# A fused network on one NeuronCore: modulation blocks ahead of first products, a ring filled two blocks further, and RWKV's first mix without the difference

## The reference, cut to what matters

```python
for i in range(DEPTH_2):                       # 4
    shift, scale, gate = modulation(c, mod_w[i], mod_b[i])     # silu(c) @ mod_w[i] + mod_b[i]
    h = modulate(rmsnorm(x, norm_g[i]), shift[:, None], scale[:, None])
    ...                                        # the same with c_ctx for the context
    x = x + gate[:, None] * y

def rwkv_features(h, proj, with_out):
    xx = centred_shift(h) - h                  # 0.5 * (left + right neighbour) - h
    lerp = lambda n: h + xx * mu[n]
    k = lerp(2) @ w_k
    ...                                        # r from lerp(0), w from 1, v from 3, a from 4, g from 5
```

## Time and profile before

| | |
|---|---|
| runs | 3016.09, 3008.73, 3015.09 us; median 3015.09 |
| the profiled execution | 3009.6 us, its span 3007.8 us, mean granted clock 0.943 |
| PE busy | 2640.9 us, 88% of the span |
| DVE, ACT, POOL busy | 50%, 37%, 25% |
| ring blocks | 311 issues in the page, 512 KB each, 3.8 us (median) from issue to landing |
| store and reload of the stream X | 3072 KB each; the store takes 9.7 us to landing |
| HBM | 203.04 MB read, 36.70 MB written |

### The profile page before, as it was taken

How to read it: one execution, slowest core, us unless ns; L and a number is a source line. 1 busy time by engine, 2 the same in 40 slices (tenths; PEclk the granted TensorE clock), 3 DMA queues, 4 the chain that set the end, 5 groups by cost and what they waited for, 6 DMA issues and landing times. The chain is left out here.

```text
span 3007.8 us, 66771 instructions
## 1 busy us (share of the span) xinstructions
PE 2640.9 (88%) x28836; PEld 2003.8 (67%) x28836; DVE 1511.2 (50%) x2661; ACT 1127.2 (37%) x1763; POOL 762.1 (25%) x438
## 2 busy tenths in 40 slices
PE   8897899979799996888888887789999999898987
PEld 5675577847578785676767776568778655476755
DVE  4634478883642313545555544334550166525995
ACT  4533332232352333444444443234432344423323
POOL 2322200002112125545444441122223300032111
PEclk9998999999789897999999999889999999999998
DMA  4214253334434441111111100441312200044421
GB/s 149 77 57 139 86 156 100 98 90 130 152 138 165 152 142 62 40 40 51 35 35 51 45 15 24 173 162 50 126 57 71 62 1 1 29 158 138 141 88 56
DMA packets 83663, 266.38 MB, mean 89 GB/s; under 512 B 11824, under 2 KB 12848, under 8 KB 82992
## 3 DMA queue, kind: packets, MB, share of 16 engines
q1 hardware_dynamic: 74160, 236.97, 24.8%
q10 hardware_dynamic: 9216, 25.17, 2.1%
HBM read 203.04 MB, written 36.70 MB: 80 GB/s over the span
## 5 line engine op out<-in xcount | busy, mean ns | idle before, releaser
L373 PE MATMUL ps<-h_parts_conv,w_parts_one 128*128 128x512 f32 x3168 | 582.1, 344 | 43.0 <-DVE h_parts_conv L359 32.3
L373 PEld LDWEIGHTS ps<-h_parts_conv,w_parts_one 128*128 128x128 f32 x3168 | 494.7, 191 | 137.6 <-issue 43.3
L373 PE MATMUL ps<-scratch_scan 64*64 64x64 f32 (+1 forms) x15936 | 376.1, 236 | 87.3 <-issue 48.0
L373 PEld LDWEIGHTS ps<-scratch_scan 64*64 64x64 f32 x15936 | 338.0, 137 | 132.8 <-issue 87.8
L441 POOL TENSOR_TENSOR w_parts_rwkv_out<-ring,w_parts_rwkv_out 128x1024 fp32r<-128x1024 f32 x80 | 191.1, 2391 | 807.1 <-ACT w_parts_rwkv_out L370 807.1
L441 POOL TENSOR_TENSOR w_parts_one<-ring,w_parts_one 128x1024 fp32r<-128x1024 f32 x82 | 202.8, 2475 | 716.9 <-ACT w_parts_one L370 716.9
L370 ACT ACTIVATE scratch_scan<-ps 128x384 f32<-128x384 f32 x560 | 241.3, 493 | 369.5 <-PE ps L373 225.1
L367 DVE SCALAR_TENSOR_TENSOR scratch_conv<-scratch_conv,vec 128x256 f32<-128x256 f32 (+1 forms) x672 | 337.4, 575 | 0.5
L373 PE MATMUL ps<-h_parts_attn,w_parts_rwkv_out 128*128 128x512 f32 (+1 forms) x1536 | 331.0, 374 | 5.8 <-DVE h_parts_attn L367 5.8
L373 PEld LDWEIGHTS ps<-h_parts_attn,w_parts_rwkv_out 128*128 128x128 f32 x1536 | 265.3, 190 | 65.0 <-issue 14.9
L373 PE MATMUL ps<-h_parts_block,w_parts_one 128*128 128x512 f32 x960 | 241.2, 409 | 19.3 <-DVE h_parts_block L359 17.1
(11 more groups left out here) (215 smaller groups left out, 3353.1 us busy)
## 6 DMA issues: line engine op xcount, KB each, us to landing
ring<-in_weights SPq DMA_DIRECT2D x311, 512.0 KB, 3.8
rwkv_spill<-scratch_conv ACTq DMA_DIRECT2D x64, 384.0 KB, 2.3
stream<-rwkv_spill SPq DMA_DIRECT2D x64, 384.0 KB, 3.6
scratch_conv<-scratch_conv SPq DMA_DIRECT2D x128, 103.1 KB, 2.2
scratch_conv<-scratch_conv SPq DMA_DIRECT2D x128, 67.4 KB, 2.0
x_spill<-stream SPq DMA_DIRECT2D x2, 3072.0 KB, 9.7
y_spill<-scratch_scan SPq DMA_DIRECT2D x8, 384.0 KB, 4.1
scratch_rwkv_out<-y_spill SPq DMA_DIRECT2D x8, 384.0 KB, 6.4
```

Of the source, the lines that this page charges most:

```text
L373: return nc.tensor.matmul(o, l, r, start=start, stop=stop)
```

## The change

Five things change.

1. `tile_product` takes three numbers, `mods=(front, behind, col)`: so many modulation blocks before the first k-step, then one behind each of the first `behind` k-steps. Numbers (front, behind) by stage: out1 (2, 2), gate1 (2, 0), conv0 (6, 2), convout0 (6, 2), rkvg (4, 4), rwkvout (2, 0), attn_qk (6, 2), attnout (2, 2), conv1 (6, 2). Before, one block stood behind each of the first k-steps: four in out1, gate1, rwkvout, attn_qk and attnout, eight in the others. In gate1 and rwkvout one more pair stands behind a later product; in attn_qk the pairs behind the first two products go. MODS places the blocks in the ring to match, and in gate1 the first two split blocks come ahead of the direct ones.
2. The ring is filled up to START + SLOTS + 2 at the ends of in1, out1, gate1, add_products' stages, attn_g and attnout (not at the ends of conv0, conv1 and rkvg); before, up to START + SLOTS.
3. RWKV's first mix is `LF = h * (1 - mu) + sum * (0.5 * mu)`: ACT writes `h * (1 - mu)` into LF with a scale per channel, DVE adds the second term. The difference is formed for all eight tiles behind the first group.
4. The wait for `normed` before the first turning of values goes.
5. Three semaphores of the convolution layers are shared by both, with a base added to the numbers waited for.

The diff, cut:

```diff
-MODS = {"out1": {1: 4, 3: 2, 5: 2}, "gate1": {3: 4, 5: 2, 7: 2},
+MODS = {"out1": {1: 4, 3: 2, 5: 2}, "gate1": {3: 2, 5: 2, 6: 2, 7: 2},
...
-    stage("gate1", [("w_ple_proj", 0, 0), ("w_ple_proj", 0, 1)] + [("w_ple_gate", 0, m) for m in range(8)])
+    stage("gate1", [("w_ple_gate", 0, m) for m in range(2)] + [("w_ple_proj", 0, m) for m in range(2)] + [("w_ple_gate", 0, m) for m in range(2, 8)])
...
+            mod_blocks(pe, mods[0], mods[2])
             for k in range(DT):
...
-                if k < mods[0]:
-                    mod_blocks(pe, 1, mods[1])
+                if k < mods[1]:
+                    mod_blocks(pe, 1, mods[2])
...
-                R.supply(sp, RINGT, weights, START["out1"] + SLOTS)
+                R.supply(sp, RINGT, weights, START["out1"] + SLOTS + 2)
...
-                    if m in (2, 4):
+                    if m in (2, 3, 4):
                         mod_blocks(pe, 2, 5 * 512)
...
+                def first_mix(k):
+                    v.wait_ge(in_hi, base_shifted + 4 * k + 4)
+                    for j, (a, b, c) in enumerate(HALF):
+                        v.wait_ge(dve_chain.sem, dve_chain.base + dve_chain.n - 1 + j)
+                        stt(LF[:, k, a:b], XX[:, k, a:b], HALFMU[:, k:k + 1], LF[:, k, a:b], ALU.mult, ALU.add).then_inc(l_ready, 1)
+
+                def differences():
+                    for k in range(DT):
+                        for a, b, c in HALF:
+                            n, o = b - a, hoff[c]
+                            dve_chain.inc(stt(XX[:, k, a:b], XX[:, k, a:b], 0.5, HP[:, k, o:o + n], ALU.mult, ALU.subtract))
                     dve_chain.wait(v)
...
                 mod_gain(1, 2)
+                dlink(vts(HALFMU, V("rwkv_mu_2", groups[0][0] * DT, DT), 0.5))
+                vts(RESTMU, V("rwkv_mu_2", groups[0][0] * DT, DT), -1.0, 1.0, ALU.mult, ALU.add).then_inc(rest_ready, 1)
...
+                    for j, (p, q, c) in enumerate(HALF):
+                        a.wait_ge(in_hi, base_shifted + 4 * k + j + 1)
+                        if k == 0:
+                            a.wait_ge(rest_ready, 1)
+                        act(LF[:, k, p:q], HP[:, k, hoff[c]:hoff[c] + q - p], ACT.Copy, scale=RESTMU[:, k:k + 1]).then_inc(in_hi, 1)
...
-                                 mods=(4, MODS_3) if n == 0 else (0, 0))
-                    if n < 2:
-                        mod_blocks(pe, 2, MODS_3)
+                                 mods=(6, 2, MODS_3) if n == 0 else (0, 0, 0))
...
                         if kinds[n - 1][1] == 0:
                             pe.wait_ge(mods_added, 10)
-                            pe.wait_ge(normed, NT_)
```

More of the change, by code:

```diff
@@ L106 @@
 IN_ORDER = [base + m for base in (0, 12, 8, 16, 4, 20) for m in range(4)]
-MODS = {"out1": {1: 4, 3: 2, 5: 2}, "gate1": {3: 4, 5: 2, 7: 2},
+MODS = {"out1": {1: 4, 3: 2, 5: 2}, "gate1": {3: 2, 5: 2, 6: 2, 7: 2},
         "conv0": {1: 8}, "convout0": {1: 8, 3: 2, 4: 2, 5: 2, 6: 2},
-        "rkvg": {1: 8, 11: 2, 13: 2, 15: 2, 16: 2}, "rwkvout": {1: 4, 3: 2, 5: 2},
-        "attn_qk": {1: 6, 2: 2, 11: 2, 13: 2, 15: 2, 17: 2}, "attnout": {1: 4, 6: 2, 10: 2}, "conv1": {1: 8}}
+        "rkvg": {1: 8, 11: 2, 13: 2, 15: 2, 16: 2}, "rwkvout": {1: 2, 2: 2, 3: 2, 5: 2},
+        "attn_qk": {1: 8, 11: 2, 13: 2, 15: 2, 17: 2}, "attnout": {1: 4, 6: 2, 10: 2}, "conv1": {1: 8}}
 def weight_plan():
@@ L452, in part_block_vector, with tile_product @@
                 done["part"] += 1
-        def tile_product(pe, o, width, area=None, start=True, stop=True, fresh=None, used=None, mods=(0, 0)):
+        def tile_product(pe, o, width, area=None, start=True, stop=True, fresh=None, used=None, mods=(0, 0, 0)):
             j = done["take"]
@@ L1011, in _ @@
                         bring(sp, base_hi)
-                    R.supply(sp, RINGT, weights, min(b for b in [*START.values(), NB] if b > START[stage]) + SLOTS)
+                    R.supply(sp, RINGT, weights, min(b for b in [*START.values(), NB] if b > START[stage]) + SLOTS + 2)
                 @block.scalar
@@ L1041, in _ @@
                                      fresh=(split_low, base_low, 1) if split and m == 0 else None,
-                                     mods=(mods[0][3], mods[0][1]) if mods and m == 0 else (0, 0))
+                                     mods=(*mods[0][3], mods[0][1]) if mods and m == 0 else (0, 0, 0))
                         for third, col, rows, _n, later, _at, turn_at in mods:
@@ L1094, in _ @@
                 sp.dma_start(PE_, pT.rearrange("(k p) t -> p k t", p=P)).then_inc(loads, 16)
-                R.supply(sp, RINGT, weights, START["conv0"] + SLOTS)
+                R.supply(sp, RINGT, weights, START["conv0"] + SLOTS + 2)
             @block.tensor
@@ L1102, in _ @@
                     tile_product(pe, PS[:, (m % 2) * 512:(m % 2) * 512 + 512], TX,
-                                 fresh=(split_low, base_low, 1) if m == 0 else None, mods=(4, 5 * 512) if m == 0 else (0, 0))
+                                 fresh=(split_low, base_low, 1) if m == 0 else None, mods=(2, 0, 5 * 512) if m == 0 else (0, 0, 0))
                     if m == 0:
@@ L1206, in two_blocks @@
         z_summed, centred, z_scaled, silued, gated_ = (sem(n) for n in ("z_summed", "centred", "z_scaled", "silued", "gated_"))
[L1208 removed]
+        conv_sems = tuple(sem(n) for n in ("a_read", "b_read", "gate_read", "pe_taps", "taps_added", "padded",
+                                           "s_free", "diag_ready", "stacked"))
         def conv_layer(layer, j_, width):
@@ L1312, in _ @@
                                          fresh=input_fresh if m == 0 and part == 0 else None,
-                                         mods=(8, 5 * 512) if m == 0 and part == 0 else (0, 0))
+                                         mods=(6, 2, 5 * 512) if m == 0 and part == 0 else (0, 0, 0))
                             if m >= 1 and part == 1:
@@ L1430, in conv_layer @@
             add_products(f"convout{j_}", width, lambda m, c: MODL[:, layer, 16 + m, c:c + 1],
-                         2 if j_ == 0 else 0, split=(silu_and_high, gate_and_low), mods=[(3, 4 * 512, MOD_ROWS, 8, (), 0, 1), (4, 5 * 512, MOD_ROWS, 0, (2, 3, 4, 5), 6, 6)] if j_ == 0 else (),
+                         2 if j_ == 0 else 0, split=(silu_and_high, gate_and_low), mods=[(3, 4 * 512, MOD_ROWS, (6, 2), (), 0, 1), (4, 5 * 512, MOD_ROWS, (0, 0), (2, 3, 4, 5), 6, 6)] if j_ == 0 else (),
                          sums=([sa[:, n, 0:width] for n in range(2)], sb_[:, 0, 0:width]))
@@ L1517, in _ @@
                         neighbours(k - 1)
-                        lerp(groups[0][0], k - 1)
+                        first_mix(k - 1)
                     if k >= 2:
@@ L1545, in _ @@
                                      used=h_used if (kind, q, m) == prods[-1] and e + 1 < len(groups) else None,
-                                     mods=(8, 5 * 512) if n == 0 else (0, 0))
+                                     mods=(4, 4, 5 * 512) if n == 0 else (0, 0, 0))
                         n += 1
@@ L2621, in two_blocks @@
                      split=plain_split([YR[:, k, :] for k in range(DT)], TT, lambda k: (in_loaded[k], 16 * (NPAIR + 1))),
-                     bring=bring_back, stream=lambda m: (in_loaded[m], 16 * (NPAIR + 2)), sums=([sq[:, 0, :], sq[:, 1, :]], acc), mods=[(7, 4 * 512, take(256), 4, (2, 4), 5, 6)])
+                     bring=bring_back, stream=lambda m: (in_loaded[m], 16 * (NPAIR + 2)), sums=([sq[:, 0, :], sq[:, 1, :]], acc), mods=[(7, 4 * 512, take(256), (2, 0), (1, 2, 4), 5, 6)])
         NQ, NKV = 16, 8
@@ L2658, in _ @@
                 sp.dma_start(ROPE.rearrange("p a t -> p (a t)"), rope).then_inc(loads, 16)
-                R.supply(sp, RINGT, weights, START["attnout"] + SLOTS)
+                R.supply(sp, RINGT, weights, START["attnout"] + SLOTS + 2)
             @block.tensor
@@ L2898, in _ @@
                 sp.dma_start(X.rearrange("p k t -> p (k t)"), x_dram).then_inc(loads, 16)
-                R.supply(sp, RINGT, weights, START["conv1"] + SLOTS)
+                R.supply(sp, RINGT, weights, START["conv1"] + SLOTS + 2)
             @block.scalar
@@ L2930, in _ @@
                                      fresh=(split_low, base_low + DT * half, 1) if m == 0 else None,
-                                     mods=(4, 4 * 512) if m == half == 0 else (0, 0))
+                                     mods=(2, 2, 4 * 512) if m == half == 0 else (0, 0, 0))
                     if m in (2, 4):
```

27 lines of the change are left out of this document (12 added, 15 removed).

## The result

Four runs of the changed kernel took 2964.77 to 2973.52 us, median 2966.71; beside them the kernel before has a median of 3014.64. The ratio is 0.985, interval 0.984 to 0.987: 1.5% faster. Predicted was 2967. The profiled execution has a span of 2963.6 us (before 3007.8, 44.2 more).

What follows compares the result with a forecast made beforehand. TensorE was taken as the bound, so its standing still was what counted. Stage terms summed to 46.0 us, taken as 45.6, giving 2964.0 from the profiled execution or 2969.5 from the median; forecast 2967, range 2951 to 2986.

Steps and rivals of the forecast that it cites:

- gate1, rwkvout: First products no longer wait for late modulation blocks: gains of 11.8 us in gate1 and 9.1 us in rwkvout.
- no wait for the ring: Sign for gate1: TensorE waits for no ring block, and the third product starts at 300.
- attnout: Four blocks loaded at the stage's start remove the first product's hole of 4.97 us: gain 8.0 us, bounds 6 and 9.5.
- my second case: attnout: TensorE's clock, high when the stage begins, holds, but third weights land behind the stream: gain 8.6 us.
- rkvg's first mix: VectorE's pace per k-step falls from 4.98 to 3.93 us in rkvg's first product: gain 6.9 us, bounds 5 and 8.5.
- attn_v: The needless 3.93 us wait before the first transposition goes, and the next product runs faster: gain 5.4 us.
- attn_qk: Front blocks five and six land behind the 3 MB store and hold k-step 0: loss of 2.3 us.
- conv1: Four blocks run in the hole, two more follow, then k-steps of 0.7: gain 3.4 us, bounds 2 and 4.
- out1: A pair of blocks in the starting hole and an earlier clock: gain 1.9 us, bounds 1.2 and 2.5.
- the clock rival: Clock falls in thinned first products of convout0 and conv0, 3.4 us each: total 2974; chance 0.15.
- rival of late blocks: Front blocks come as late in conv0, convout0 and conv1 as in attn_qk, some 12 us after issue: 2982; chance 0.09.
- The "slower" one: Clock, once low in a thinned first product, stays low through the whole next one: 3030; chance 0.02.

Runs made afterwards that it cites:

- e9: Changed kernel with gate1's direct blocks ahead of its split ones again and out1 filling the ring only to START + SLOTS: 2979.79 us, +13.1.
- e10: Changed kernel with rwkvout's four modulation blocks behind k-steps 0 to 3 and pairs behind products 2 and 4, as before: 2977.89 us, +11.2.
- e2: Changed kernel with no modulation blocks in front of first products, the same number one behind each of the first k-steps: 2973.94 us, +7.2.
- e1: Changed kernel with the ring filled only up to START + SLOTS at the five places: 2986.97 us, +20.3.
- e7: Changed kernel with two more ring blocks issued ahead of the 3 MB store in attn_qk and ahead of the reload in attnout: 2973.26 us, +6.5.
- e3: Changed kernel with RWKV's first mix formed from the difference again, as in the kernel before: 2974.30 us, +7.6.
- e4: Changed kernel with the wait for all 24 normalisations ahead of the first turning of values put back: 2976.72 us, +10.0.
- e8: Changed kernel with four blocks in front and four behind k-steps, not six and two, in conv0, convout0 and conv1: 2963.97 us, -2.7.
- e11: Changed kernel with four front, four behind in conv0, convout0, conv1, attn_qk; six ring blocks ahead of attn_qk's store, two ahead of attnout's reload: 2958.86 us.
- e12: As e11, but with seven further ring blocks ahead of attn_qk's store, including the third product's weights: 2960.38 us, ratio 0.983 to the kernel before.

## Why the prediction was right

*gate1, rwkvout* (20.9 predicted; 22.2 and 21.8 measured): right in size and in what goes, the wait for a late third block; e9 and e10 take each of them away alone. I had ascribed gate1's to blocks that "are in the ring before the stage begins". They were not, and "no wait for the ring", one of my signs, did not come (5.08 and 1.54 us); the third product was on time all the same. e2 shows that standing in front was worth 0.4 and 0.7. In gate1 the order in the ring, with its depth, did it (e9). In rwkvout it is the order and the smaller number of blocks together (e10).

*attnout* (8.0; 7.3 and 7.6): the clock held, as in my second case, and the third weights were late by 1.87 us behind the reload. e1 shows that the deeper ring is the whole of it; in e7, where two blocks go ahead of the reload, the stage is 2.3 shorter.

*rkvg's first mix* (6.9; 7.3 and 7.5): right in pace and size; e3. The rest of rkvg, which I had at nothing, with 0.3 for the clock, lost 1.0 and 1.3. It comes at the two changes of group, where no instruction of TensorE changed, and it is hardly chance: from the second product to behind the second change the twelve profiles with the new mix lose 1.0 to 1.8 us against the kernel before, the one with the old mix (e3) 0.4. At the first change the stretch between two roundings takes 10.1 us at a granted clock of 0.86 in the first profile, 9.2 at 0.95 before and 9.3 at 0.94 in e3 (columns as in the earlier trace rows; changed kernel, then before):

```profile
873.94:884.04 10.10, 10.10 (x52) 8.75 (x52) 9.12 (x14) 1.87 (x2) 2.40 (x1) 0.86 0.61 213
```

```profile
899.62:908.80 9.18, 9.18 (x52) 8.04 (x52) 9.13 (x14) 1.87 (x2) 2.41 (x1) 0.95 0.70 237
```

So the new mix seems to have a price of about 1 us, paid mostly in clock; it rests on one profile of e3, and why the clock rises later there is not shown.

*attn_v* (5.4; 5.65 twice): right, e4. The 0.2 over it is that TensorE no longer stands between the two matmuls ahead and the turnings: the turnings now start 0.85 us behind them, while the two took 1.02 to their end before the wait began.

*attn_qk* (-2.3; -2.4 and -1.8): right in place and size, though three front blocks were loaded and not four.

*conv1* (3.4; 0.3 and 0.2): mis-sized, and outside its bounds of 2 to 4. Unfolded, my sum has the front end at 2743.2, 7.2 us behind VectorE's first instruction of the stage (2736.01), and then "k-steps of 0.7 and two blocks", 6.8. Measured, the front ended 7.9 behind it, the k-steps and two blocks took 8.8, and the stage began 0.7 late where I had 0.35. So the step that failed most is the k-steps of 0.7: behind the ring waits the first two took 1.65 and 1.28 us and the block between them 1.08. With four and four (e8, e11, e12) conv1 is 2.3 to 3.3 shorter.

*out1* (1.9; 3.8, 4.0): of the first 1.2 lies at the end of in1, where four matmuls took 3.50 us before and 2.33 now with the same code; 2.6 is the stage's. By the table's rule the eleven profiles with this code give 2.2 to 4.0, all above my 1.9, and e2 gives 1.2, e1 0.4.

*convout0, conv0*: the clock rival had 0.15 with a price of 3.4 each. It came true in convout0 in five of nine profiles, at 1.8 to 3.1. In conv0 it did not: there the k-steps, held back by late blocks in front, follow each other without a gap, and what its two profiles differ by (1.3 us) is how early the clock rose in the front blocks. The row of convout0 in the earlier trace rows, which I weighed against the one of rkvg, was of denser work and could not bear on the thinned product; 0.15 was too low a chance for this half of the rival. Of the rival of late blocks something is seen in conv1, 2.6 us of waits and not the 12 that it was priced by. The "slower" one did not come even in convout0: in all nine profiles the 10 us behind that rounding have the clock 1.00.

So the mechanism was right in the five large terms, and the total is closer than its terms: in the first profile conv1 (3.1 under), conv0 and rkvg's rest (1.0 each), attnout (0.7) and the stages without a term (1.0) stand against out1 (1.9 over), convout0 (1.3), rwkvout (0.9), gate1 and rkvg's first product (0.4 each). That these cancel to 1.4, and that the median fell on 2967 to 0.3 us, is luck. The good ends of my bounds, with 1.3 and 1.2 for conv0 and convout0, add up to 55 and not 56; the range does not hang on it.

## What to carry to other kernels

Ask of each block not where it stands on the consumer, but whose release its slot waits for and what stands ahead of its transfer in the queue; here a bulk transfer issued first at a stage's start delayed the weight blocks behind it in two stages, and moving some of them ahead (e7) only moved the wait in attn_qk: all that the first product needs had to precede it (e11). In front of a product put only as many blocks as have landed by then: in conv1 and attn_qk each further one held back steps that were ready. Compare two kernels by a repeated landmark (here 210 roundings), not by sums of waits or busy time; and profile the same kernel twice before crediting a stage with 1 to 3 us.

## What the runs showed of the hardware

The same instructions cost 1 to 3 us more or less from one execution to the next. In two places the granted clock shows it: convout0 up to 3.1 us (0.83 or 1.00), and convout1, where the way from the second rounding to the third took 40.4 us at a mean of 0.75 in the first profile and 38.0 at 0.82 in e4. The end of in1 differs by 1.2 us in four matmuls. The scan (last rounding of rkvg to the first of rwkvout) took 759.1 to 764.9 us over fourteen profiles with one code; there the mean granted clock does not tell them apart (0.95 at 760.9 and at 764.9), and the cause is open. After a hole of 3.93 us a product of 48 matmuls took 10.26 in one execution and 10.81 in another, 8.73 without the hole. In convout0's two profiles above, the first two k-steps took 2.29 and 1.62 us where the clock held later on, 1.96 and 1.32 where it fell: it had risen earlier there. What makes it rise sooner or later in one execution is left open.
